# Two masking products side by side: the causal mask of two neighbouring score tiles, put behind the second tile's products

## The chip, the cores and the metric

The kernel runs on one core of one Trainium2 chip. The metric is the device time of one execution in microseconds (us). Five engines take part. TensorE (PE in the profile, PEld for its weight loads) multiplies 128-row tiles from the on-chip memory SBUF and writes the sums to one of eight PSUM banks. VectorE (DVE), ScalarE (ACT) and GpSimd (POOL) do the element-wise work. SyncE (SP) issues most of the DMAs. The engines run by themselves and wait for one another through semaphores.

## The reference, cut to what matters

Two transformer blocks run one after the other on 512 tokens of width 1024. The first block has two layers: a differential attention with an MLP, and a latent ("MLA") attention with an MLP. The second block mixes convolution, pooling and two small attentions, and is not touched here. The two attentions of the first block are what the change is about:

```python
# differential attention, 8 heads; each head has two score matrices (components c = 0, 1)
s = einsum('bqhcd,bkhcd->bhcqk', q_blk, k) * scale
s = where(causal_mask, s, -inf);  p = softmax(s, -1)
a = p[:, :, 0] - lam * p[:, :, 1]          # then a @ v

# latent attention, 8 heads
s = (einsum('bqhd,bkhd->bhqk', qn, k_nope) + einsum('bqhr,bkr->bhqk', qr, k_rope)) * scale
s = where(causal_mask, s, -inf);  p = softmax(s, -1)   # then p @ v
```

Every matrix product is made nearly exact in float32: each operand is split into a high and a low part, and two or three products are summed in one PSUM bank.

## The kernel before, in words

The scores of a head are made as four tiles, one for each block of 128 queries, called A, B, C and D in this document. Because of the causal mask tile `i` needs only the keys of the blocks 0 to `i`, so the tiles are 128, 256, 384 and 512 keys wide (the narrowest is computed 256 wide). Tile `i` of a group goes to PSUM bank `(T + i) % 4`: the four tiles of a group fill four banks, and the next group of four needs each of them again.

A tile of the differential attention is two products (`diff_scores`, L658 and L659) and one masking product (`mask_later`, L645). The masking product multiplies a 128x128 bf16 identity (the weights) by a 128x128 bf16 mask and adds the result to the 128 columns of the tile on the diagonal. It is the last of the tile and raises `tile_done`. A tile of the latent attention is two products L774 and L775, one product in two pieces at L776, and the same masking product (`mla_scores`). The scores are made negated, so that the row maximum is found with a minimum.

What follows a tile is the same in both attentions. VectorE waits for the tile's `tile_done` and takes the row minimum (`negmin`, L1525 in the differential attention, L1717 in the latent one). ScalarE waits for that and takes the exponential (`probs` L1055, `mla_probs` L1202), which also gives the row sum and raises `bank_free` of the tile's bank. TensorE waits for `bank_free` (`bank_ready`, L502) before the first product of the next tile in that bank. `tile_done` counts upwards, tile after tile.

The order of the work on each engine is written out by hand. In the differential attention TensorE does for head n, in `diff_step`: the four tiles of component 0 of head n+1, the turn of an earlier output (L693), the product with v of head n-1 (`weighted`, L683), the transposes of head n's probabilities (L672, which wait for `a_done`, raised by L1546), and the four tiles of component 1 of head n+1. VectorE does for head n: `rinv` and two more small steps (L1535 to L1539), which need the last exponential of the head's component 1; the four row minima of component 0 of head n+1; the combination of the two components (`probs`, L1546); some steps for earlier heads (L1560, L1552, L1555); the four row minima of component 1 of head n+1. ScalarE takes the exponentials, and between them copies the transposed probabilities (L1064) and the outputs (L1071).

In the latent attention (`mla_step`) TensorE does for head n: tiles A and B of head n+1, the transposes of head n (L672), tiles C and D of head n+1, the product with v (L786). VectorE does: `rinv` and the normalisation of head n (L1724, L1728), minima A and B, one step for the head before (L1422), minima C and D. Before head 0 of either attention all its tiles are made in one go. After each attention the output projection follows at once (L534), with weights that are loaded and split long before.

Of the kernel before, what the change touches and what calls it, by code (L numbers as in the profile page):

```python
# [20 lines left out]
P = 128  # L21
# [38 lines left out]
C, T = {}, {}  # L60
# [61 lines left out]
def build(nc, wst, xT, gains, cos, sin, ident_in, mask_in, lam, pT_in, tab_in, buckets_in, pool_w_in, pool_fix_in, outT):  # L122
    ctx = ExitStack()
    with ctx:
        def sem(name):
            return ctx.enter_context(nc.semaphore(name))
# [139 lines left out]
        ps = [ctx.enter_context(nc.psum_tensor(f"ps{b}", [P, S], F32)) for b in range(8)]  # L266
# [9 lines left out]
        tile_done = sem("tile_done")  # L276
# [215 lines left out]
        def _(pe):  # L492
# [6 lines left out]
            def bank_ready(t, per=0, i=0):  # L499

                if not isinstance(i, int) or t // 4 + (per // 4) * i > 0:
                    pe.wait_ge(bank_free[t % 4], t // 4 + (per // 4) * i)  # L502
# [140 lines left out]
            def mask_later(out):  # L643

                return pe.matmul(out, ident_b[:, :], mask_b[:, :], start=False, stop=True)  # L645

            def diff_scores(par, half, comp, first=False):

                pe.wait_ge(stage_full[par][comp], 96 * (half + 1))
                if first:  # L650
                    pe.wait_ge(pad_zero, 2 * par + comp + 1)
                for i in range(QT):
                    n = 8 * par + 4 * comp + i
                    bank_ready(T["diff"] + n, 16, half)
                    b, q = ps[(T["diff"] + n) % 4], slice(P * i, P * i + P)
                    wide = max(P * (i + 1), 2 * P)

                    pe.matmul(b[:, 0:wide], stage[par][:, comp, 0, q], stage[par][:, comp, 1, 0:wide], start=True, stop=False)  # L658
                    pe.matmul(b[:, 0:wide], stage[par][:, comp, 0, q], stage_k_lo[par][comp][:, 0:wide],  # L659
                              start=False, stop=False)  # L660
                    mask_later(b[:, q]).then_inc(tile_done, 1)

            def transposes(src, ready, n):

# [31 lines left out]
            def diff_step(par, half, first=0, scores=True):  # L696

                n = 2 * half + par
                if scores:
                    diff_scores(1 - par, half + par, 0, first=n == 0 if isinstance(n, int) else False)  # L700
                if first >= 3 and scores:
                    turn(o_raw[1 - par], n - 3, X["diff_o"] + n - 3)
                if first >= 1:
                    weighted(pT[1 - par], v_tok, n - 1, n - 1, oc_done)
                if not scores:
                    turn(o_raw[1 - par], n - 3, X["diff_o"] + n - 3)
                transposes(probs[par][:, 0, :], lambda j, i: (a_done, 4 * n + j + 1), n)
                if scores:
                    diff_scores(1 - par, half + par, 1, first=n == 0 if isinstance(n, int) else False)

            pe.wait_ge(dve_const, 5)
            diff_scores(0, 0, 0, first=True)
            diff_scores(0, 0, 1, first=True)
            for n in range(3):
# [18 lines left out]
            c, t = C["dkv"], T["dkv"]  # L733
# [7 lines left out]
            c, t = C["ukv"], T["ukv"]  # L741
# [17 lines left out]
            c, t = C["uq"], T["uq"]  # L759
# [5 lines left out]
            def mla_scores(par, n, tiles):  # L765

                if 0 in tiles:
                    pe.wait_ge(mla_full[par], 80 * (n // 2 + 1) if isinstance(n, int) else 80 + 40 * (n - par))
                for i in tiles:
                    bank_ready(T["mla"] + i, 4, n)  # L770
                    b, w, q = ps[(T["mla"] + i) % 4], P * (i + 1), slice(P * i, P * i + P)
                    wide = max(w, 2 * P)

                    pe.matmul(b[:, 0:wide], mla_qr[par][:, q], mla_kr[:, 0:wide], start=True, stop=False)  # L774
                    pe.matmul(b[:, 0:wide], mla_qr[par][:, q], mla_kr_lo[:, 0:wide], start=False, stop=False)  # L775
                    pe.matmul(b[:, 0:w], mla_qn[par][:, q], k_nope[:, n, 0:w], start=False, stop=False)  # L776
                    mask_later(b[:, q]).then_inc(tile_done, 1)

            def mla_weighted(par, n):

# [9 lines left out]
            def mla_step(par, n, scores=True):  # L790
                if scores:
                    mla_scores(1 - par, n + 1, (0, 1))
                transposes(mla_probs[par], lambda j, i: (pn_done, 4 * n + j + 1), HEADS + n)
                if scores:
                    mla_scores(1 - par, n + 1, (2, 3))
                mla_weighted(par, n)

            pe.wait_ge(kr_zero, 1)
            pe.wait_ge(kr_full, 96)
            mla_scores(0, 0, range(QT))  # L800
            mla_step(0, 0)
            with pe.Fori(0, HEADS // 2 - 1) as i:
# [7 lines left out]
            c, t = C["w_in"], T["w_in"]  # L810
# [1567 lines left out]
```

## Time and profile before

| | us |
|---|---|
| median of 3 runs | 1896.39 |
| lowest, highest | 1894.56, 1898.91 |
| the profiled execution's own time | 1895.68 |
| its span (first to last instruction) | 1893.9 |
| TensorE busy in the span | 1846.5 (97%) |
| mean granted TensorE clock | 0.99 |
| differential attention | from 154.8 to 227.3 of the span |
| latent attention | from 715.2 to 776.6 of the span |

The profile is one execution. Ends of TensorE's instructions are modelled, so distances between the starts of two neighbouring instructions say what one of them costs, not its duration: the products overlap in the array. An idle time in square brackets stands in front of an instruction and names what ended it.

### The profile page before, as it was taken

The numbers are of one execution on the slowest core, as the hardware profiler recorded it, in microseconds if no ns is written. First come the engines' busy times: TensorE is split into PE (matmuls) and PEld (weight loads), VectorE is DVE, ScalarE is ACT, GpSimd is POOL, SyncE is SP. The second block draws the span as 40 slices with busy tenths as digits, with TensorE's granted clock in tenths as the row PEclk, the third lists the DMA queues.
The fourth block names the chain that finished last, engine by engine and source line by source line (L and its number), as shares of the span: only waits on it lengthen the run. The fifth ranks groups of instructions, "written<-read, shape, count | busy, mean of one in ns | idle before, by whom it ended". The sixth has DMA issues, their size and how long they took to land.

```text
span 1893.9 us, 22795 instructions
## 1 busy us (share of the span) xinstructions
PE 1846.5 (97%) x8690; PEld 1504.4 (79%) x8694; DVE 914.5 (48%) x1129; ACT 613.3 (32%) x886; POOL 571.6 (30%) x365
## 2 busy tenths in 40 slices
PE   8999999999999999999999999999998999999988
PEld 6897788888888876788888888777785888888866
DVE  6745763333335765543333335597546332333364
ACT  4236722122223335422212224234435222322342
POOL 3310355141325430252324155221115210211252
PEclk9999999999999999999999999999998999999998
DMA  4434332232222234225232222311121222222221
GB/s 173 142 111 96 96 112 89 89 111 89 98 102 89 89 114 117 91 93 141 89 104 96 89 98 98 121 67 45 45 101 61 95 92 104 93 102 99 89 88 67
DMA packets 40558, 183.94 MB, mean 97 GB/s; under 512 B 5512, under 2 KB 12200, under 8 KB 21416
## 3 DMA queue, kind: packets, MB, share of 16 engines
q1 hardware_dynamic: 38224, 179.26, 28.0%
q10 hardware_dynamic: 2264, 3.72, 1.0%
q8 instruction: 47, 0.77, 0.2%
q14 instruction: 23, 0.19, 0.0%
HBM read 161.99 MB, written 3.67 MB: 87 GB/s over the span
## 4 chain that ended last, share of the span: by engine, by line
PE 86%; DVE 8%; ACT 2%; POOL 2%; issue 1%; DMA 1%; SPq 0%; DVEq 0%; ACTq 0%; POOLq 0%
PE ps L495 23%; PE ps L496 23%; PE ps L497 23%; PE ps L545 3%; PE ps L534 3%; PE ps L535 3%; PE ps L672 1%; DVE xb L1422 1%; PE ps L863 1%; PE ps L881 1%; PE ps L786 1%; PE ps L776 1%; DVE wlo L1416 1%; DVE probs L1546 1%; PE ps L579 1%
## 5 line engine op out<-in xcount | busy, mean ns | idle before, releaser
L1416 DVE TENSOR_TENSOR wlo<-raw,whi 128x2048 fp32r<-128x2048 f32 x142 | 352.1, 2480 | 324.4 <-ACT whi L972 324.0
L972 ACT ACTIVATE whi<-raw 128x2048 fp32r<-128x2048 f32 x149 | 284.3, 1908 | 382.6 <-PE ps L497 272.6
L495 PE MATMUL ps<-xb,whi 128*128 128x512 f32 x1024 | 402.8, 393 | 2.8 <-DVE wlo L1416 1.6
L497 PE MATMUL ps<-xb,wlo 128*128 128x512 f32 x1024 | 400.0, 391 | 0.0
L496 PE MATMUL ps<-xb,whi 128*128 128x512 f32 x1024 | 399.9, 391 | 0.0
L495 PE MATMUL ps<-xa_hi,whi 128*128 128x512 f32 x788 | 308.7, 392 | 3.2 <-DVE wlo L1416 3.2
L497 PE MATMUL ps<-xa_hi,wlo 128*128 128x512 f32 x788 | 307.8, 391 | 0.0
L496 PE MATMUL ps<-xa_lo,whi 128*128 128x512 f32 x788 | 307.7, 390 | 0.0
L495 PEld LDWEIGHTS ps<-xb,whi 128*128 128x128 f32 x1024 | 193.3, 189 | 45.9 <-issue 3.3
L497 PEld LDWEIGHTS ps<-xb,wlo 128*128 128x128 f32 x1024 | 193.1, 189 | 40.8
L496 PEld LDWEIGHTS ps<-xb,whi 128*128 128x128 f32 x1024 | 193.4, 189 | 39.8 <-issue 0.2
L2121 POOL TENSOR_TENSOR u_sq<-u_tmp 128x512 f32<-128x512 f32 x64 | 66.7, 1042 | 385.8 <-DVE u_tmp L1626 385.8
L495 PEld LDWEIGHTS ps<-xa_hi,whi 128*128 128x128 f32 x788 | 148.8, 189 | 35.3 <-DVE wlo L1416 4.5
L497 PEld LDWEIGHTS ps<-xa_hi,wlo 128*128 128x128 f32 x788 | 148.5, 188 | 31.2
L496 PEld LDWEIGHTS ps<-xa_lo,whi 128*128 128x128 f32 x788 | 148.7, 189 | 30.5
L1607 DVE TENSOR_TENSOR h<-ps,h 128x512 f32<-128x512 f32 x80 | 54.0, 690 | 188.8 <-PE ps L497 144.0
L1626 DVE SCALAR_TENSOR_TENSOR u_tmp<-ps,rstd_f 128x512 f32<-128x512 f32 x64 | 43.4, 690 | 143.3 <-PE ps L497 141.5
L2214 POOL TENSOR_TENSOR hid_t<-silu_t,up_t 128x512 f32<-128x512 f32 x22 | 28.3, 1286 | 236.8 <-ACT silu_t L1372 120.5
L534 PE MATMUL ps<-xa_hi,whi 128*128 128x512 f32 x188 | 73.5, 391 | 2.0 <-ACT xa_hi L979 1.9
L535 PE MATMUL ps<-xa_hi,wlo 128*128 128x512 f32 x188 | 73.2, 389 | 0.0
L2124 POOL TENSOR_TENSOR xb<-u_sq,xb 128x512 fp32r<-128x512 f32 x32 | 70.4, 2201 | 2.5
L2124 POOL TENSOR_TENSOR xa_lo<-u_sq,xa_hi 128x512 fp32r<-128x512 f32 x32 | 68.4, 2139 | 2.5
(311 smaller groups left out, 2516.9 us busy)
## 6 DMA issues: line engine op xcount, KB each, us to landing
raw<-wst SPq DMA_DIRECT2D x149, 1024.0 KB, 4.8
stage<-qk_split SPq DMA_DIRECT2D x64, 128.0 KB, 2.4
h<-xT ACTq DMA_DIRECT2D x4, 512.0 KB, 8.0
stage_k_lo<-qk_split SPq DMA_DIRECT2D x32, 64.0 KB, 2.0
mla_qn<-q_nope SPq DMA_DIRECT2D x8, 256.0 KB, 2.7
mla_v<-v_tok SPq DMA_DIRECT2D x8, 256.0 KB, 2.7
outT<-h SPq DMA_DIRECT2D x8, 256.0 KB, 2.0
bias_scratch<-bias_rows ACTq DMA_DIRECT2D x1, 1536.0 KB
```

Source lines behind the costliest of these rows:

```text
L495: pe.matmul(out, lhs_hi, rhs_hi, start=first, stop=False)
L496: pe.matmul(out, lhs_hi, rhs_lo, start=False, stop=False)
L497: return pe.matmul(out, lhs_lo, rhs_hi, start=False, stop=last)
L534: pe.matmul(out, w_hi[:, k, m], xhi[:, k, :], start=(k == 0), stop=False)
L535: pe.matmul(out, w_lo[:, k, m], xhi[:, k, :], start=False, stop=False)
L545: mm = pe.matmul(ps[(t0 + a) % 4][:, :], w_hi[:, k, m], xlo[:, k, :], start=False, stop=(k == kt - 1))
L972: act.activation(whi[slot][:, :], raw[slot][:, :], ACT.Copy).then_inc(whi_done, 1)
L1416: dve.tensor_tensor(wlo[slot][:, :], raw[slot][:, :], whi[slot][:, :].bitcast(F32), ALU.subtract).then_inc(wlo_done, 1)
L1607: dve.tensor_tensor(h[:, k, :], ps[t % 4][:, :], h[:, k, :], ALU.add).then_inc(bank_free[t % 4], 1)
L1626: dve.scalar_tensor_tensor(out=u_tmp[:, a, :], in0=ps[tt % 4][:, :], scalar=0.0, in1=rstd_f[:, :], op0=ALU.max, op1=ALU.mult)\
L2121: pool.tensor_tensor(u_sq[:, a, :], u_tmp[:, a, :], u_tmp[:, a, :], ALU.mult).then_inc(hid_sq, 1)
L2124: pool.tensor_tensor(hlo[:, j, :], u_sq[:, a, :], hhi[:, j, :].bitcast(F32), ALU.subtract)\
```

## The change

The masking product of a tile no longer stands behind the tile's own products. When the products of the second tile of a pair (B, or D) have been issued, a new helper `mask_pair` issues the masking products of both tiles, one behind the other, first A then B (first C then D). Both have the same weights. Each still raises `tile_done` by one, in the same order of tiles. The number of products and of weight loads stays the same. The second tile's wait for its bank now stands ahead of the first tile's masking product. The third kind of place where the identity is used, in the second block, is untouched.

```diff
+            def mask_pair(t, i):
+
+                for j in range(2):
+                    mask_later(ps[(t + j) % 4][:, P * (i + j):P * (i + j) + P]).then_inc(tile_done, 1)
+
             def diff_scores(par, half, comp, first=False):
...
                     pe.matmul(b[:, 0:wide], stage[par][:, comp, 0, q], stage_k_lo[par][comp][:, 0:wide],
                               start=False, stop=False)
-                    mask_later(b[:, q]).then_inc(tile_done, 1)
+                    if i % 2 == 1:
+                        mask_pair(T["diff"] + n - 1, i - 1)
...
                     pe.matmul(b[:, 0:w], mla_qn[par][:, q], k_nope[:, n, 0:w], start=False, stop=False)
-                    mask_later(b[:, q]).then_inc(tile_done, 1)
+                    if i % 2 == 1:
+                        mask_pair(T["mla"] + i - 1, i - 1)
```

The order on TensorE, in the differential attention: the four tiles of component 1 of head 2, which follow the transposes of head 1 (`stage` holds the queries and the high part of the keys, `stage_k_lo` the low part). Before:

```order
L658 MATMUL ps<-stage_97 128x256 [waits bank_free0,stage_full01]
L659 MATMUL ps<-stage_k_lo_100,stage_97 128x256
L645 MATMUL ps<-mask_b,ident_b 128x128
L658 MATMUL ps<-stage_97 128x256 [waits bank_free1]
L659 MATMUL ps<-stage_k_lo_100,stage_97 128x256
L645 MATMUL ps<-mask_b,ident_b 128x128
L658 MATMUL ps<-stage_97 128x384 [waits bank_free2]
L659 MATMUL ps<-stage_k_lo_100,stage_97 128x384
L645 MATMUL ps<-mask_b,ident_b 128x128
L658 MATMUL ps<-stage_97 128x512 [waits bank_free3]
L659 MATMUL ps<-stage_k_lo_100,stage_97 128x512
L645 MATMUL ps<-mask_b,ident_b 128x128
```

The same place of the changed kernel, whose lines are 5 further down:

```order
L663 MATMUL ps<-stage_97 128x256 [waits bank_free0,stage_full01]
L664 MATMUL ps<-stage_k_lo_100,stage_97 128x256
L663 MATMUL ps<-stage_97 128x256 [waits bank_free1]
L664 MATMUL ps<-stage_k_lo_100,stage_97 128x256
L645 MATMUL ps<-mask_b,ident_b 128x128 x2
L663 MATMUL ps<-stage_97 128x384 [waits bank_free2]
L664 MATMUL ps<-stage_k_lo_100,stage_97 128x384
L663 MATMUL ps<-stage_97 128x512 [waits bank_free3]
L664 MATMUL ps<-stage_k_lo_100,stage_97 128x512
L645 MATMUL ps<-mask_b,ident_b 128x128 x2
```

The masks of tiles A and C have moved behind two more products and behind the wait for the next bank; the masks of B and D stand where they stood.

On TensorE in the latent attention, tiles C and D of head 1, with the rows taken away and put in (`k_nope` and `mla_kr` are the keys, `mla_qr` the rotated part of the queries, bank numbers shown):

```order
+L780 MATMUL ps1<-mla_kr_168,mla_qr1_167 128x384 [waits bank_free1]
+L781 MATMUL ps1<-mla_kr_lo_169,mla_qr1_167 128x384
+L782 MATMUL ps1<-k_nope_158,mla_qn1_165 128x384
+L780 MATMUL ps2<-mla_kr_168,mla_qr1_167 128x512 [waits bank_free2]
+L781 MATMUL ps2<-mla_kr_lo_169,mla_qr1_167 128x512
+L782 MATMUL ps2<-k_nope_158,mla_qn1_165 128x512
 L645 MATMUL ps1<-mask_b_68,ident_b_67 128x128
-L774 MATMUL ps2<-mla_kr_168,mla_qr1_167 128x512 [waits bank_free2]
-L775 MATMUL ps2<-mla_kr_lo_169,mla_qr1_167 128x512
-L776 MATMUL ps2<-k_nope_158,mla_qn1_165 128x512
 L645 MATMUL ps2<-mask_b_68,ident_b_67 128x128
```

The mask of tile C (bank `ps1`) now follows all of tile D's products (bank `ps2`), and the two masks are neighbours. On the other engines no instruction moves.

## Rows read from the trace of the kernel before

**Rows 1.** The page: busy us, share of the span, instructions.

```profile
PE 1846.5 (97%) x8690; PEld 1504.4 (79%) x8694; DVE 914.5 (48%) x1129; ACT 613.3 (32%) x886; POOL 571.6 (30%) x365
```

**Rows 2.** Waits, differential attention, 154 to 225: total us, times, longest.

```profile
DVE negmin L1525 <- PE ps L645: 5.3, 10, 1.8
```

**Rows 3.** Waits, latent attention, 712 to 772.

```profile
DVE negmin L1717 <- PE ps L645: 19.7, 23, 1.5
```

**Rows 4.** Timeline of TensorE, head 3: start us, us, engine, line, operation.

```profile
183.11 0.23 PE L645 MATMUL ps<-mask_b,ident_b 128*128 128x128 bf16 x1
183.15 0.36 PE L658 MATMUL ps<-stage 128*128 128x256 f32 x1
183.35 0.28 PE L659 MATMUL ps<-stage_k_lo,stage 128*128 128x256 f32 x1
...
183.95 0.23 PE L645 MATMUL ps<-mask_b,ident_b 128*128 128x128 bf16 x1
...
184.54 0.23 PE L645 MATMUL ps<-mask_b,ident_b 128*128 128x128 bf16 x1
```

**Rows 5.** Timeline of TensorE, first score tile, no mask ahead of it.

```profile
154.84 0.28 PE L658 MATMUL ps<-stage 128*128 128x256 f32 x1
154.95 0.28 PE L659 MATMUL ps<-stage_k_lo,stage 128*128 128x256 f32 x1
```

**Rows 6.** Timeline of VectorE and ScalarE, head 3, tiles C and D.

```profile
184.22 0.56 DVE L1525 TENSOR_REDUCE negmin<-ps 128x1 f32<-128x384 f32 x1
184.81 0.69 DVE L1525 TENSOR_REDUCE negmin<-ps 128x1 f32<-128x512 f32 x1
185.53 0.69 ACT L1055 ACTIVATE probs<-ps,negmin 128x512 f32<-128x512 f32 x1
```

**Rows 7.** Timeline of TensorE and VectorE, head 5, tiles C and D.

```profile
201.54 0.23 PE L645 MATMUL ps<-mask_b,ident_b 128*128 128x128 bf16 x1
...
201.39 0.55 DVE L1525 TENSOR_REDUCE negmin<-ps 128x1 f32<-128x384 f32 x1
...
201.85 0.68 DVE L1525 TENSOR_REDUCE negmin<-ps 128x1 f32<-128x512 f32 x1
```

**Rows 8.** Timeline, head 0, tile D of component 1, and its minimum.

```profile
158.33 0.50 PE L658 MATMUL ps<-stage 128*128 128x512 f32 x1
...
158.90 0.23 PE L645 MATMUL ps<-mask_b,ident_b 128*128 128x128 bf16 x1
...
159.17 0.69 DVE L1525 TENSOR_REDUCE negmin<-ps 128x1 f32<-128x512 f32 x1 [0.39 <-PE ps L645]
```

**Rows 9.** Timeline, transposes of head 0, and weight loads (PEld) of head 3's last ones.

```profile
163.31 0.59 PE L672 MATMUL ps<-ident,probs 128*128 128x128 f32 x3 [1.77 <-DVE probs L1546]
...
190.60 0.42 PEld L672 LDWEIGHTS ps<-ident,probs 128*128 128x128 f32 x4 [0.34 <-DVE probs L1546]
```

**Rows 10.** Stretches: length; PE, PEld, DVE, ACT, POOL busy; PEclk; DMA share, GB/s.

```profile
164.00:169.00 5.00, 4.79 (x23) 3.75 (x24) 2.22 (x6) 2.83 (x9) 0.00 (x0) 0.66 0.66 149
170.00:222.00 52.00, 49.82 (x358) 39.71 (x357) 43.31 (x110) 41.29 (x133) 16.30 (x16) 1.00 0.59 141
```

**Rows 11.** Timeline of TensorE, latent attention, transposes of a steady head.

```profile
743.60 1.60 PE L672 MATMUL ps<-ident,mla_probs 128*128 128x128 f32 x10
```

**Rows 12.** Timeline of VectorE, latent attention, the normalisation ahead of those transposes.

```profile
742.05 0.55 DVE L1728 TENSOR_SCALAR mla_probs<-mla_probs,rinv 128x256 f32<-128x256 f32 x2
```

**Rows 13.** Timeline, latent attention, last head: tiles C and D, then transposes.

```profile
768.16 0.22 PE L645 MATMUL ps<-mask_b,ident_b 128*128 128x128 bf16 x1
...
769.59 0.22 PE L645 MATMUL ps<-mask_b,ident_b 128*128 128x128 bf16 x1
...
769.85 0.69 DVE L1717 TENSOR_REDUCE negmin<-ps 128x1 f32<-128x512 f32 x1 [0.88 <-PE ps L645]
...
772.01 1.70 PE L672 MATMUL ps<-ident,mla_probs 128*128 128x128 f32 x10
```

**Rows 14.** Timeline of TensorE, latent attention, transposes of its head 0.

```profile
721.38 1.63 PE L672 MATMUL ps<-ident,mla_probs 128*128 128x128 f32 x10 [0.46 <-DVE mla_probs L1728]
```

## The prediction

> **What bounds the kernel now.** The first view to read is the busy time of the engines: TensorE is busy for 97% of the span and the next engine for 48% [rows 1]. As a rule, then, a nanosecond of TensorE is a nanosecond of the kernel. The waits of the two attentions are the second view, because there the rule may fail. In the differential attention VectorE waits 10 times for a masking product, 5.3 us in all [rows 2]; in the latent one 23 times, 19.7 us [rows 3]. Such a wait costs nothing if VectorE has time to spare, and all of it if TensorE later waits for VectorE. The timelines tell which. In the differential attention TensorE's transposes wait for VectorE's combination of the probabilities: 1.77 us at head 0, and at head 3 the weight loads of the last four still stand idle for 0.34 us [rows 9]. The loop there is closed by this chain: combination, last transposes, component 1's tiles, minima, exponentials, minima of the next head, combination. In the latent attention's steady heads the combination's counterpart, the normalisation, starts at 742.05, and the transposes that read it start at 743.60 without a wait [rows 11, 12]: TensorE is the bound, with over a microsecond of slack on the other side. Its two ends are different. TensorE waits 0.46 us for the first head's probabilities [rows 14], and the last head's transposes at 772.01 follow at once on a chain that begins at the mask of tile D, 769.59 [rows 13].
>
> **What the edit gives TensorE.** In head 3 a mask starts at 183.11 and the next tile's first product 0.04 later, at 183.15; its second product starts 0.20 after that, at 183.35 [rows 4]. Without a mask ahead, the same two products start 0.11 apart, 154.84 and 154.95 [rows 5]. So a mask that has a float32 tile behind it takes 0.04 + 0.09, about 0.12 us since the rows are rounded: most of it is the next weight load, which the short mask cannot cover. After the edit one of each pair's masks has the other mask behind it. No row shows what such a slot costs. Its ends are 0.04 (the start after a mask above) and 0.12 (a float32 load as badly covered as now). I take 0.06: it has half the columns of the products that start 0.11 apart [rows 5], and its weights have half the width. The gain is 0.12 - 0.06 = 0.06 us for each pair that lies on TensorE's path, with ends 0 and 0.08.
>
> The TensorE page of the Trainium skill ("TensorE: Matmul & The Clock Gate", Weight-path perf modes) says that weights which are not float32 are loaded by a faster way, which speaks for the low end. Its section on the back-to-back issue gap gives some 81 ns for a stream of loads and products of 128 columns; as an estimate by that page the gain would be 0.04 us a pair, and the sum below 0.3 us higher. No run here shows it yet.
>
> **What the edit takes from the chain behind the tiles.** The mask of tile C moves behind tile D's products. In head 3 mask D starts at 184.54. Before it stand three masks, at 0.12 each; after the edit the mask of C stands behind A's and B's alone, at 0.06 + 0.12. So it starts at 184.54 - 0.36 + 0.18 = 184.36, against 183.95 now, and mask D at 184.42. The minimum of tile C starts 0.27 after its mask, now 184.22 [rows 6], then 184.63. The minimum of D cannot start sooner than 0.46 after C's (201.39 to 201.85, where nothing is waited for, [rows 7]): 185.09, against 184.81 [rows 6]. The exponential of tile D, at 185.53, starts 0.03 after that minimum ends, and everything behind it is late by the same 0.28 us: `rinv`, the minima of the next head, the combination, the transposes. The masks of A and B have slack, since ScalarE is still copying when A's minimum is done.
>
> In head 5 VectorE is later for reasons of its own and the delay smaller: mask D at 201.54 puts mask C at 201.54 - 0.18 = 201.36, its minimum at 201.63, against 201.39: 0.24 us [rows 7]. Heads 2 and 3 are of the first kind. Head 4 comes out between, 0.27. Heads 5, 6 and 7 are of the second. The sum of the six is 0.28 x 2 + 0.27 + 0.24 x 3 = 1.55 us.
>
> Head 0 has both its components exposed. Component 0 is late by 0.28 as above, and with it the bank that tile D of component 1 waits for: its first product goes from 158.33 to 158.61. From there to a mask it is 158.90 - 158.33 = 0.57, so mask C starts at 159.18, its minimum at 159.45 and D's at 159.91, against 159.17 [rows 8]: 0.74 us. The component 0 tiles of the later heads cost nothing: VectorE reads them only after `rinv`.
>
> Head 1's component 1 runs at half clock. The granted clock is 0.66 in the mean of 164 to 169 [rows 10], so TensorE ran at 1.2 instead of 2.4 GHz for some 3.4 of these 5 us, after it had stood idle for 1.77 us. If that stretch stays where it is in time, work that comes 0.74 us later does up to half of that, 0.37, less of itself in it. Against this stands head 1's own delay of 0.24. I take 0, with ends -0.1 and +0.3.
>
> In the latent attention the end of the last head is a straight chain. Mask D at 769.59 becomes mask C at 769.59 - 0.12 = 769.47; its minimum starts 0.26 later and D's 0.46 after that, at 770.19, against 769.85 [rows 13]: 0.34 us, and the transposes, the product with v and the output projection all move with it. The first head ends in the same chain and TensorE waits for it already [rows 14]: 0.34 again. In the steady heads the same 0.34 goes into the slack [rows 11, 12] and costs nothing; with the slack gone it would cost 0.34 for each of six heads. Of the 16 pairs 13 lie on TensorE's path (not the last pairs of the first and the last head, nor the one behind which TensorE waits), and give 13 x 0.06 = 0.78. The sum is 0.68 - 0.78 = -0.1 us, with ends -0.4 and +0.7.
>
> DMAs, and the waits of SyncE for `tile_done`, hang on the last tile of each group, whose mask moves by 0.1 us at most. No queue is passed. Behind both attentions TensorE is the bound and nothing takes the delay back.
>
> **The sum.** 0.74 + 0 + 1.55 - 0.1 = 2.2 us. The profiled execution took 1895.68, so it would take 1897.9. The median of the runs is 0.71 above that: 1896.39 + 2.2 = 1898.6 us, or 0.12% more.
>
> **The rivals.**
>
> First, the delay is absorbed: VectorE and ScalarE find the time again somewhere in a head. The idle 0.34 before the last transposes [rows 9] speaks against it, since it says who waits for whom; for it speaks that only 5.3 us of waits for masks are seen [rows 2]. Then what remains is TensorE's gain, 0.8 to 1 us in the latent attention and perhaps as much in the other: 1895.1.
>
> Second, on the far side: a further stretch at half clock. TensorE is already idle for 1.77 us before the first transposes and drops to 1.2 GHz behind it [rows 9, 10]. The edit lengthens the idle pieces around heads 0 and 1. One more stretch of 3.4 us loses up to 3.4 / 2 = 1.7 us, two lose 3.4: 1900.3 to 1902. It decides as soon as one of the idle pieces outside that stretch grows enough to bring the clock down; from 170 to 222 the granted clock is 1.00 throughout, so the short pieces there do not do so now [rows 10]. The same page of the skill warns, in its section on psum-queue depth-cycling, of a clock that oscillates when TensorE idles briefly and often between groups of products. The trace shows none of it from 170 to 222.
>
> Third, the change does not do what it says: both masks have the same weights, but the second weight load stays in the program, and a pair may save nothing. Then the latent attention costs 0.7 instead of -0.1, the mask of C comes 0.06 later throughout, and the sum is 2.2 + 0.8 + 0.5 = 3.5: 1899.9.
>
> **How the numbers follow.** The forecast, a small loss of 1.5 to 3 us, gets 0.64; absorbed 0.12; a further half-clock stretch 0.12; no saving 0.08; something else 0.04. A measurement of this kernel tells about 0.2%, 3.8 us, from no change. "Slower by over 0.2%" takes two thirds of the clock rival, a quarter of the third and the upper tail of the forecast, since the runs of before alone lie 4 us apart: 0.08 + 0.02 + 0.09, with the rest of something else 0.21. "Faster by over 0.2%" would need 3.8 us, while all 48 pairs at their best give 48 x 0.08 = 3.8: 0.03. The range runs from the absorbed case to nearly two lost clock stretches, 1895.0 to 1901.6.
>
> **What would show it right or wrong.** In the profile after, the two neighbouring masks should start 0.06 apart, and the first product of tile D 0.18 rather than 0.22 after C's second one. The minimum of tile C should start some 0.4 later after its head's first product than now, that of D some 0.25 to 0.3. From the first score tile to the output projection the differential attention should take about 74.8 us instead of 72.5, the latent one 61.3 instead of 61.4. The first figure falls if ScalarE's exponential of D starts no later in its head than now. The second falls if the transposes of steady heads begin to wait. The sum falls if the granted clock shows more stretches at half than now, or fewer.

## The result and the profile after

The changed kernel takes 1899.23 us in the median of 20 runs (1897.89 to 1900.83), the kernel before 1896.48 in the same jobs (20 runs, 1894.56 to 1898.91). The medians are 2.75 us apart. The ratio is 1.0016, with a 95% interval of 1.0009 to 1.0022, which is 1.7 to 4.2 us. The forecast of a small loss (1898.6 us, within 0.2% of before) came out. The terms of its sum did not all do so, and the experiments below are about them. The two executions that were profiled took 1895.68 us (before) and 1900.14 us (after), so the profiles lie further apart than the medians.

The page of the changed kernel, against [rows 1], looks the same. Nothing can be learnt from it.

```profile
PE 1849.2 (97%) x8694; PEld 1506.4 (79%) x8694; DVE 912.3 (48%) x1129; ACT 612.8 (32%) x886; POOL 571.2 (30%) x365
```

The waits do change. First VectorE's for a mask in the differential attention (154 to 226 us; total us, times, longest), against [rows 2], then in the latent one (714 to 775), against [rows 3], and behind them the three largest waits of TensorE's weight loads in the differential attention:

```profile
DVE negmin L1532 <- PE ps L645: 8.4, 12, 2.2
...
DVE negmin L1724 <- PE ps L645: 20.6, 9, 2.7
...
PEld ps L663 <- ACT probs L1062: 8.6, 21, 0.8
PEld ps L678 <- DVE probs L1553: 6.0, 13, 1.9
PEld ps L645 <- issue: 4.4, 16, 0.3
```

The same rows of the kernel before for the weight loads read:

```profile
PEld ps L672 <- DVE probs L1546: 7.3, 17, 1.9
PEld ps L645 <- issue: 7.1, 32, 0.3
PEld ps L658 <- ACT probs L1055: 2.4, 7, 0.5
```

VectorE's wait for masks grew in both stages. In the first one TensorE's loads then stand 6.2 us longer behind the banks that ScalarE frees, and 1.3 us less behind `probs` and 2.7 us less ahead of the masks: 2.2 us more idle time of the loads, though not every part of it stops the products.

Head 3 of the changed kernel (start us, us, engine, line, operation), against [rows 4] and [rows 6]:

```profile
184.88 0.36 PE L663 MATMUL ps<-stage 128*128 128x256 f32 x1
185.08 0.28 PE L664 MATMUL ps<-stage_k_lo,stage 128*128 128x256 f32 x1
185.20 0.28 PE L663 MATMUL ps<-stage 128*128 128x256 f32 x1
...
185.44 0.29 PE L645 MATMUL ps<-mask_b,ident_b 128*128 128x128 bf16 x2
185.53 0.42 PE L663 MATMUL ps<-stage 128*128 128x384 f32 x1
185.79 0.34 PE L664 MATMUL ps<-stage_k_lo,stage 128*128 128x384 f32 x1
185.97 0.39 PE L663 MATMUL ps<-stage 128*128 128x512 f32 x1
...
186.44 0.29 PE L645 MATMUL ps<-mask_b,ident_b 128*128 128x128 bf16 x2
```

```profile
186.70 0.56 DVE L1532 TENSOR_REDUCE negmin<-ps 128x1 f32<-128x384 f32 x1 [0.37 <-PE ps L645]
187.18 0.68 DVE L1532 TENSOR_REDUCE negmin<-ps 128x1 f32<-128x512 f32 x1
...
187.89 0.69 ACT L1062 ACTIVATE probs<-ps,negmin 128x512 f32<-128x512 f32 x1
```

The group's first product starts at 182.78 in before and at 184.88 here. Measured from it, mask C comes at 1.56 us, before at 1.17; its minimum at 1.82, before 1.44; D's minimum at 2.30, before 2.03; the exponential at 3.01, before 2.75. So tile C is 0.38 to 0.39 later in its head, and everything from D's minimum on 0.26 to 0.27.

Where the stages end is read from three rows of TensorE: the output projection behind the differential attention, the latent attention's first score product, and the projection behind that. Before:

```profile
227.28 0.48 PE L534 MATMUL ps<-xb,whi 128*128 128x512 f32 x1
...
715.19 0.28 PE L774 MATMUL ps<-mla_kr,mla_qr 128*128 128x256 f32 x1
...
776.63 0.48 PE L534 MATMUL ps<-xa_hi,whi 128*128 128x512 f32 x1
```

and after, with the first score product ahead of them:

```profile
155.75 0.28 PE L663 MATMUL ps<-stage 128*128 128x256 f32 x1
...
229.69 0.48 PE L534 MATMUL ps<-xb,whi 128*128 128x512 f32 x1
...
717.58 0.28 PE L780 MATMUL ps<-mla_kr,mla_qr 128*128 128x256 f32 x1
...
778.94 0.47 PE L534 MATMUL ps<-xa_hi,whi 128*128 128x512 f32 x1
```

| us | before | after | difference | forecast |
|---|---|---|---|---|
| ahead of the first score product | 154.84 | 155.75 | +0.91 | 0 |
| differential attention | 72.44 | 73.94 | +1.50 | +2.3 |
| between | 487.91 | 487.90 | 0 | 0 |
| latent attention | 61.44 | 61.35 | -0.09 | -0.1 |
| behind it | 1117.26 | 1119.40 | +2.14 | 0 |
| span | 1893.9 | 1898.3 | +4.4 | +2.2 |

Two thirds of the difference between these two profiles lie in stages whose code the change does not touch. Of these the stretch ahead of the first score product is within its spread: the same code takes from 153.07 to 156.20 us there in the fourteen profiles of this document. The part behind the latent attention needs a closer look, which comes below. A table by stage is therefore worth more here than the time, and each experiment below is read by it first. "diff" and "latent" stand for the second and fourth row.

### The profile page after: what moved, and what is told of

Same layout as the page of the kernel before. It is cut to its first block, busy times and chain, and to the rows that moved or that the text cites. A ratio compares the mean times of both kernels' runs of the same rounds, so it can differ in the third digit from the quotient of the medians.

```text
span 1898.3 us, 22799 instructions
## 1 busy us (share of the span) xinstructions
PE 1849.2 (97%) x8694; PEld 1506.4 (79%) x8694; DVE 912.3 (48%) x1129; ACT 612.8 (32%) x886; POOL 571.2 (30%) x365
## 4 chain that ended last, share of the span: by engine, by line
PE 87%; DVE 7%; ACT 2%; POOL 2%; issue 1%; DMA 1%; SPq 0%; ACTq 0%; DVEq 0%; POOLq 0%
PE ps L495 23%; PE ps L496 23%; PE ps L497 23%; PE ps L545 3%; PE ps L534 3%; PE ps L535 3%; PE ps L678 1%; DVE xb L1429 1%; PE ps L870 1%; PE ps L888 1%; PE ps L782 1%; PE ps L793 1%; DVE wlo L1423 1%; PE ps L579 1%; POOL rstd_t L2067 1%
```

## Experiments

### One stage at a time, and the pairs put elsewhere

**e1** keeps the pairs in `mla_scores` alone, **e2** in `diff_scores` alone.

```diff
 (e1, in diff_scores)
-                    if i % 2 == 1:
-                        mask_pair(T["diff"] + n - 1, i - 1)
+                    mask_later(b[:, q]).then_inc(tile_done, 1)
```

> Pairs of masks in the latent attention alone; the differential attention as before. My theory (0.057 us gained by TensorE for each of 13 pairs, 0.35 us lost at each end): the latent attention takes 61.35 us against 61.44 of before, the differential one 72.4, and the time is that of before within 0.3 us of -0.1. The rival that the change costs something outside the two stages: the time is 1 us or more above that of before although both stages show nothing.

> Pairs of masks in the differential attention alone. My theory: the differential attention takes 73.9 us against 72.4 of before, the latent one 61.4, and the time is 1.5 us above that of before. Rival, that the measured 2.75 us have a part outside both stages: the time is 2.5 us or more above, with the same 1.5 in the stage.

e1: diff 72.09, latent 61.36; median 1895.78 against 1896.83, ratio 0.9997 (0.9988 to 1.0006). e2: diff 74.07, latent 61.45; 1899.21, ratio 1.0011 (1.0002 to 1.0020). The loss is the differential attention's, and the latent attention's small gain is there in the profile (61.35 to 61.36 in e1, in after and in its repetition **e5**, 61.44 to 61.45 in every kernel with the old latent order and nothing ahead of it), far below what the time can tell. e2's stage is 1.6 us longer, as its theory said. Its median is 2.4 us above that of before, between the 1.5 of the theory and the 2.5 of the rival, so the time does not decide between them.

**e3** leaves the pairs only where, by the prediction, nobody waits: component 0 of the heads behind the first, and in the latent attention all but the last two tiles of the first and last head. For this the last round of the loop over heads is written out.

```diff
+                    if comp == 1 or alone:
+                        mask_later(b[:, q]).then_inc(tile_done, 1)
+                    elif i % 2 == 1:
+                        mask_pair(T["diff"] + n - 1, i - 1)
...
+                    if i >= 2 and isinstance(n, int) and n in (0, HEADS - 1):
+                        mask_later(b[:, q]).then_inc(tile_done, 1)
...
-            with pe.Fori(0, HEADS // 2 - 1) as i:
+            with pe.Fori(0, HEADS // 2 - 2) as i:
...
+            mla_step(1, HEADS - 3)
+            mla_step(0, HEADS - 2)
```

> Pairs only where no chain hangs on the first mask: component 0 of heads 1 to 7 in the differential attention, and all of the latent attention but the C and D tiles of its first and last head. My theory: the differential attention keeps its 72.4 us (within 0.2), the latent one loses both its ends' costs and takes 61.44 - 0.057 x 13 = 60.7 us; the time is 0.7 us below that of before. The rival, that a late mask costs wherever it stands: the differential attention takes 0.7 us more, half of what the whole change costs it.

**e4** pairs the masks of tiles A and B alone, in both attentions:

```diff
+                    if i == 1:
+                        mask_pair(T["diff"] + n - 1, 0)
+                    elif i >= 2:
+                        mask_later(b[:, q]).then_inc(tile_done, 1)
```

> Only tiles A and B are paired, in both attentions; C and D as before. My theory (mask C is what is late): the differential attention takes no more than 72.4 us, perhaps 0.3 less since mask C comes 0.06 earlier; the latent one 61.44 - 0.057 x 7 = 61.0. The rival, that mask A is late too: the differential attention takes 0.2 us more for each head, 1 us or more in all.

e3: diff 72.07, latent 61.10; 1895.68, ratio 0.9994 (0.9985 to 1.0003). e4: diff 70.91, latent 61.01; 1896.06, ratio 0.9996 (0.9987 to 1.0005). In both the loss of the differential attention is gone. In e4 heads 2 and 3 step by 7.95 us (from the exponential of tile D in one head to that in the next), where they step by 8.03 in before and 8.30 in the changed kernel: the pair of A and B gives a little in these heads, and the pair of C and D takes it and more. So the pair of C and D is the cause, and with the rows of head 3 above this is the delay of tile C. The 70.91 is not a gain of the edit: its profile has no stretch at half clock in head 1, and e9 below, with the old order and no such stretch either, takes 70.88. In e4 TensorE waits three times, 3.3 us in all, for the DMA that brings the low part of the keys, and in e9 not once, so nothing of what A and B gave in the first heads is seen at the stage's end. The last of the three:

```profile
208.31 0.38 PE L663 MATMUL ps<-stage 128*128 128x256 f32 x1 [0.89 <-DMA stage_k_lo<-qk_split]
```

The latent stage of e4 gives the expected 61.0. That of e3 misses its 60.7: the heads written out of the loop run 7.48 and 7.41 us where the same heads ran 7.24 and 7.31 in the loop. So the heads written out took 0.3 us more. In the second of them TensorE waits 0.21 us for ScalarE's copy of the transposed probabilities (758.89 us in e3), which it does not do in e1; why was not tested.

**e6** goes the other way and puts all four masks of a differential group behind tile D.

```diff
+                for j in range(4):
...
+                    if i == 3:
+                        mask_pair(T["diff"] + n - 3, 0)
```

> All four masks of a group behind tile D, in the differential attention alone; the latent attention as before. My theory: the masks of A and B are now late too, and the minima start with A's after all products: about 0.7 us later at the exponential of D, and the minima of component 0 another 0.3 late, since they can start only when its tile D is made. So some 0.9 us for each of heads 1 to 7 less what is absorbed, and 2 for head 0: the differential attention takes 78 to 81 us and the time is 6 to 9 us above that of before. The rival, that the loss comes from the longer wait for a bank ahead of the mask and is paid once: 76 us or less.

diff 78.75, latent 61.45; 1903.81, ratio 1.0041 (1.0029 to 1.0054). Stage and time agree here: +6.3 us and +7.2. VectorE's waits for masks are 14.0 us in e6 (152 to 226), against 8.4 with pairs and 5.3 before, and the heads from head 2 on step by 9.0 to 9.1 us, about 1 us more than before in heads 2 and 3 and 0.3 to 0.8 more in the later ones:

```profile
DVE negmin L1531 <- PE ps L645: 14.0, 16, 2.9
```

### Where 0.24 us a head went: GpSimd and a small step of VectorE

By when the exponential of tile D starts in component 1, with the same origin in each head, the changed kernel is later than before by 0.93, 0.91, 1.18, 1.45, 1.77, 1.74, 1.81 and 1.81 us in heads 0 to 7. At the stage's end it is 1.50. So heads 2 to 4 add 0.27 to 0.32 each as forecast, and heads 5 to 7 nothing instead of 0.24 each. Inside those heads the delay is there (the exponential of D starts 3.02 us behind the group's first product, before 2.78). Something behind the exponentials gives it back. In the kernel before, VectorE's combination begins with `coef`, a step on 4 columns. Heads 3 and 5, and GpSimd at the second (start, length):

```profile
186.56 0.22 DVE L1537 SCALAR_TENSOR_TENSOR coef<-rinv,neg_lam,rowsum 128x4 f32<-128x4 f32 x1
...
203.59 0.54 DVE L1537 SCALAR_TENSOR_TENSOR coef<-rinv,neg_lam,rowsum 128x4 f32<-128x4 f32 x1
...
203.07 1.04 POOL L2092 TENSOR_TENSOR sq_tmp<-o_raw 128x512 f32<-128x512 f32 x1
```

The same step takes 0.54 us where GpSimd squares an output at the same time, and both end within 0.02 us of each other (204.13 and 204.11). So it is in heads 4, 6 and 7. Over the eight heads of before it takes 221, 222, 223, 224, 489, 537, 533 and 541 ns. In the changed kernel everything ahead of it is later, and GpSimd's square is nearly over:

```profile
206.24 0.29 DVE L1544 SCALAR_TENSOR_TENSOR coef<-rinv,neg_lam,rowsum 128x4 f32<-128x4 f32 x1
...
205.48 1.04 POOL L2099 TENSOR_TENSOR sq_tmp<-o_raw 128x512 f32<-128x512 f32 x1
```

That is the longest of the eight; the others take 221 to 232 ns. A shorter `coef` makes the next head's tiles sooner, and head by head this is the missing term: 0.27 less in head 4 against the 0.24 of head 5 (measured -0.03), 0.25 less in head 5 (head 6: +0.07), 0.31 less in head 6 (head 7: 0), and 0.31 less in head 7 (the tail: -0.3). To test it, GpSimd's square is cut to a quarter of its width (the mean square made from it is then not the right one), in the kernel before (**e7**) and in the changed one (**e8**).

```diff
-                    pool.tensor_tensor(o_sq[:, :], o, o, ALU.mult).then_inc(sqo_done, 1)
+                    pool.tensor_tensor(o_sq[:, 0:P], o[:, 0:P], o[:, 0:P], ALU.mult).then_inc(sqo_done, 1)
```

> The kernel before, with GpSimd's square of the output (o_sq, 128x512) cut to its first 128 columns; the other columns stay zero, so the mean square that is computed from them is not the right one. My theory: in the heads 4 to 7 of before, VectorE's small step coef, which takes 0.22 us in heads 0 to 3 and 0.49 to 0.54 there, waits for the end of this GpSimd operation. With a short one it takes 0.22 everywhere and the differential attention takes 0.3 less for each of three or four heads: 71.4 us against 72.4. The rival, that coef is slow there for another reason: 0.5 us again and 72.4.

> The changed kernel with the same short square (three quarters of the square are left out). My theory: what the change cost less than I had said, in heads 5 to 7 and in the tail, was hidden by coef's wait; without that wait the pairs cost 0.24 us in each of these heads too, and the differential attention takes 2.2 to 2.5 us more than the run with the short square alone (against 1.5 with the full one). The rival, that the delay is absorbed elsewhere: 1.5 us again.

In e7, head 5:

```profile
203.72 0.40 POOL L2093 TENSOR_TENSOR sq_tmp<-o_raw 128x128 f32<-128x128 f32 x1
...
204.24 0.22 DVE L1538 SCALAR_TENSOR_TENSOR coef<-rinv,neg_lam,rowsum 128x4 f32<-128x4 f32 x1
```

`coef` is back at 0.22 in all heads. diff is 71.42 in e7 (1.02 less than before, with a stretch at half clock in head 1 in either; the median 1895.72, ratio 0.9994, 0.9985 to 1.0004) and 73.91 in e8 (as in the changed kernel; 1899.89, ratio 1.0019, 1.0009 to 1.0029, with one single run of 2070.55 us whose reason I can't name). By when the exponential of tile D starts, e8 is later than e7 by 0.90, 0.88, 1.15, 1.42, 1.76, 1.98, 2.31 and 2.59 us in heads 0 to 7: now heads 5 to 7 add their 0.22 to 0.33 too. So without this effect the pairs cost 73.91 - 71.42 = 2.49 us in this stage, and with it 1.50. The prediction had 2.3. The times of the whole kernel say nothing finer than that e7 is like before and e8 like the changed kernel.

The Trainium skill ("SBUF — State Buffer", Who interferes with whom) says that a VectorE instruction with two inputs in SBUF and a GpSimd instruction that reads SBUF exclude each other, and that the later one waits for the whole of the other. `coef` has `rinv` and `rowsum` as inputs, both in SBUF, and the rows agree: its start is recorded at 203.59, and it ends 0.02 us behind GpSimd. That it is this port, and not another resource of the two engines, no run here shows.

### Is it the chain, or only where the later work falls in time?

**e5** is the changed kernel again, **e12** the kernel before again, **e9** and **e10** the kernel before with 24 or 48 masks more, ahead of the latent attention, into a bank that is written anew afterwards.

```diff
+            for _ in range(24):
+                pe.matmul(BC[:, 0:P], ident_b[:, :], mask_b[:, :], start=True, stop=True)
```

> The changed kernel once more, for the spread of its stages. My theory: the differential attention takes 73.9 us again when its half-clock stretch of 3.4 us is there, and some 1.5 less without; the latent one 61.35. The rival, that the whole 2.75 us measured are made in the stages: 75 us or more in the differential attention.

> The kernel before once more, for a second profile of its stages. My theory: the differential attention takes 72.1 to 72.4 us with its half-clock stretch and some 1.3 less without; the part behind the latent attention lies anywhere from 1117 to 1120 us. The rival: 1117.2 us behind the latent attention as in the first profile, so that the 1119.4 of the changed kernel's profiles are its own.

> The kernel before, with 24 more masking products, one behind the other, into a bank that nobody reads, ahead of the latent attention (their result is overwritten). It measures two things. First, the slot of a mask behind a mask: my theory is 0.057 us, so 24 take 1.4 us between the two attentions. Second, what a plain delay of 1.4 us in the middle of the program does to the measured time: by my theory it adds 1.4 us, as the pairs' 1.3 to 1.5 should; by the rival (the half-clock stretches of the later stages fall at other places and last longer after such a delay) it adds 2.5 to 3.

> The same with 48 masks, 2.7 us. My theory: the time is 2.7 us above that of before. The rival: the stretches depend on where the delay leaves the program, so the addition is off from 2.7 by 1 us or more, to either side.

| | diff | latent | behind it | median us | ratio (95%) |
|---|---|---|---|---|---|
| before | 72.44 | 61.44 | 1117.26 | | |
| e12 | 72.15 | 61.45 | 1120.18 | 1897.56 | 1.0003 (0.9993 to 1.0012) |
| after | 73.94 | 61.35 | 1119.40 | 1899.23 | 1.0016 (1.0009 to 1.0022) |
| e5 | 73.73 | 61.36 | 1119.25 | 1899.91 | 1.0018 (1.0008 to 1.0027) |
| e9 | 70.88 | 61.52 | 1117.69 | 1897.98 | 1.0015 (1.0006 to 1.0024) |
| e10 | 72.48 | 61.52 | 1118.14 | 1899.83 | 1.0017 (1.0008 to 1.0026) |

First the masks themselves, the 24 of e9 in one row:

```profile
715.00 1.51 PE L799 MATMUL ps<-mask_b,ident_b 128*128 128x128 bf16 x24
```

One alone is recorded with 0.22 to 0.23 us [rows 13], so 23 further ones take 1.29: 0.056 us for each, what the prediction took (0.06). In the changed kernel two masks are recorded in one row of 0.29, again 0.06 more than one.

Then the part behind the latent attention. After the first two profiles it looked as if 1119.4 belonged to the changed kernel: the changed kernel, e2 and e5 had 1119.25 to 1119.40, the kernel before 1117.26. e12 refutes that it is the changed kernel's alone: the very kernel before has 1120.18 in another profile, and e1, whose differential attention is that of before, has 1120.29. The part takes 1117.2 to 1120.3 us in the fourteen profiles, with the same code in all. Its stretches at half clock lie in different places and add up to 29 to 36 us, and its length follows their sum: three profiles with 29 us take 1117.2 to 1117.7, four with 32 to 33 take 1118.1 to 1118.3, seven with 36 take 1119.3 to 1120.3. For instance from 1205 to 1265 (length; PE, PEld, DVE, ACT, POOL busy; PEclk; DMA share, GB/s), in before, in e12 and in after:

```profile
1205.00:1265.00 60.00, 57.59 (x292) 44.23 (x291) 46.65 (x118) 20.26 (x32) 18.42 (x4) 1.00 0.25 89
```

```profile
1205.00:1265.00 60.00, 58.15 (x280) 44.49 (x279) 45.82 (x115) 18.52 (x31) 18.37 (x4) 0.94 0.25 86
```

```profile
1205.00:1265.00 60.00, 58.15 (x287) 44.60 (x286) 45.47 (x111) 20.45 (x32) 18.46 (x4) 0.97 0.22 74
```

TensorE's granted clock was full throughout in the first and not in the two others. So the code of before can do what the changed kernel does. But it doesn't do it equally often: all four profiles with pairs of C and D in both components (after, e2, e5, e8) are among the seven with 36 us, and only three of the ten others (e1, e4, e12).

Fourteen profiles are few, but for every execution, profiled in full or not, the record gives TensorE's mean granted clock over the span, to three digits. Sorted by it, these are 103 executions of the kernel before (those that e1 to e12 were compared with, and e12 itself) and 30 of the changed kernel (after and e5):

| mean granted clock | before: executions, mean us | changed: executions, mean us |
|---|---|---|
| 0.986 | 0 | 2, 1900.7 |
| 0.987 | 0 | 9, 1900.4 |
| 0.988 | 29, 1898.2 | 13, 1899.2 |
| 0.989 | 35, 1896.9 | 6, 1898.5 |
| 0.990 | 37, 1895.6 | 0 |
| 0.991 | 2, 1894.4 | 0 |

The means are 0.9891 and 0.9878. Over 1900 us this is some 5 us more at 1.2 instead of 2.4 GHz, one and a half stretches of 3.4 us. A step of 0.001 goes with 1.3 us in the kernel before, so the lower clock stands for about 1.7 us of the difference. At the same reading the changed kernel is 1.0 (at 0.988) to 1.6 us (at 0.989) slower: that is about the stage's 1.5. The lower clock goes with the pairs of C and D in both components of the differential attention: e2 has 0.9880, e8 0.9874 against 0.9885 in e7, and e6, with all four masks behind, 0.9882 in six executions, while e1, e3, e4 and e11 together (44 executions) have 0.9892. So something in this does belong to the change, though the two profiles of before taken by themselves do not show it. Why the pairs bring it is not shown.

Can a plain delay do the same? e9 adds 23 x 0.056 plus the first mask's slot, 1.4 us by that count (1.65 between the two stages in its profile). Its median is 1.34 above that of before, but its mean is 2.15 above and its ratio says 2.8 (1.1 to 4.6): six of its eleven executions lie at 1897.6 to 1898.0 and five at 1899.2 to 1900.9. Its mean granted clock is 0.9883, against 0.9892 of before in the same job. e10 adds 2.7; its median is 3.2 above, its mean 2.95, its clock 0.9889. So e10 agrees with 1 to 1, and e9 decides neither for 1 to 1 nor for its rival of 2.5 to 3. A delay in the middle may by itself change how much is run at half clock, and the changed kernel's lower clock may be of this kind.

The stretch at half clock in the differential attention is one more such place. From 162 to 170 in after, in e4 and in e9:

```profile
162.00:170.00 8.00, 5.98 (x29) 4.44 (x29) 4.59 (x13) 5.23 (x18) 0.00 (x0) 0.79 0.58 133
```

```profile
162.00:170.00 8.00, 7.55 (x54) 5.80 (x53) 5.81 (x16) 6.13 (x22) 0.00 (x0) 1.00 0.63 144
```

```profile
162.00:170.00 8.00, 5.75 (x34) 3.81 (x34) 5.93 (x15) 6.25 (x21) 0.00 (x0) 1.00 0.59 135
```

e9's code up to this place is the kernel before's, yet it has no stretch and its stage takes 70.88 instead of 72.1 to 72.5. So the kernel before has this stretch in some executions and not in others; it costs 1.2 to 1.6 us. Ahead of it TensorE stands idle for 0.34 and then 1.77 us in before, and for 0.53, 0.64 and 1.73 in the changed kernel. All four profiles that have the change's pairs of C and D in both components (after, e2, e5, e8) have the stretch, and six of the eight with the old order of C and D have it. If the changed kernel has it always and the kernel before in about three quarters of its executions, this is worth a quarter of 1.5, 0.4 us on the medians. Four profiles cannot establish an always, and it would be a quarter of a stretch where the granted clocks ask for one and a half; the rest must lie in other stages.

### What the experiments propose

**e11** takes what each place showed: A and B paired everywhere, C and D only in latent heads 1, 2, 4 and 6, whose slack covers it and which need no code out of the loop.

```diff
+                    if i == 1 or i == 3 and pair_cd:
+                        mask_pair(T["mla"] + i - 1, i - 1)
+                    elif i >= 2 and not pair_cd:
+                        mask_later(b[:, q]).then_inc(tile_done, 1)
...
+            mla_step(0, 0, pair_cd=True)
...
+                mla_step(1, 2 * i + 1, pair_cd=True)
```

> The pairs where they can only gain: A and B in both attentions, and C and D in the latent attention's heads 1, 2, 4 and 6. My theory: differential attention 72.0 or less (70.9 if its half-clock stretch is absent, as in the run with A and B alone), latent 61.44 - 11 x 0.057 = 60.8; the time is 1 us below that of before, 0.05%. The rival: no difference to the kernel before.

The latent stage takes 60.81 us, the shortest of all. diff is 72.25, with the stretch. The median is 1896.26 against 1896.64, ratio 0.9996 (0.9987 to 1.0005): half a microsecond of gain is in the latent stage's profile, and cannot be told from nothing in the time. In the differential attention no gain is seen: the old order takes 72.09 to 72.48 with the stretch.

## Why the prediction was right, and where it was not

**The price of a mask.** Right: 0.06 was taken, and two neighbouring masks start 0.056 us apart in the latent attention (e1) and 0.067 in the differential one (e2). The first product of tile D starts 0.18 behind C's second one, as forecast (185.79 to 185.97). The rival "saves nothing" is out. The Trainium skill's 81 ns for a stream with 128 columns ("TensorE: Matmul & The Clock Gate", Back-to-back issue gap) would have given 0.04 a pair; the trace does not agree with it for these products.

**The delay of tile C and D inside a head.** Right to 0.03 us (C +0.38 for 0.41, D and its exponential +0.26 to +0.27 for 0.28, and +0.24 in heads 5 to 7).

**Head 0.** The mechanism was right, the term too small: +0.93 where 0.74 stood. The missing 0.19 is in component 0. Tile D of that first group (start us, us; the idle time before it and what ended it in brackets):

```profile
156.84 0.50 PE L663 MATMUL ps<-stage 128*128 128x512 f32 x1
...
156.84 0.19 PEld L663 LDWEIGHTS ps<-stage 128*128 128x128 f32 x1 [0.25 <-ACT v_tok L1043]
```

ScalarE is still copying `v_tok` out of the bank that tile D wants. The product starts 1.09 behind the first instead of 1.00 (0.18 behind C's second one), its own weight load is no longer covered, and its second product follows 0.34 later (157.18), in head 3 0.23. The prediction moved the masks and kept the rest of the group in place; it did not ask what frees the bank of a tile that comes sooner.

**Heads 2 to 7.** +0.27, +0.27 and +0.32 in heads 2 to 4 stood against 0.28, 0.28 and 0.27. The terms of heads 5 to 7 are the step that failed: +0.24 each was forecast, -0.03, +0.07 and 0 came, and the way to the stage's end gave back 0.3 more. The row that says so was in the trace of before: `coef` takes 0.22 us in one half of the heads and 0.54 in the other. "VectorE is later for reasons of its own" was said of head 5, and those reasons were not followed up. e7 and e8 show this term: 1.0 us.

**Head 1** at half clock took nothing in these two profiles (its step is 9.58 in before and 9.57 after): the 0 that was chosen. But with the stretch in it the same step is 9.27 in e12 and 9.36 in e5, so the code of before alone varies by 0.3 us here, and the 0 is not resolved better than that.

**The latent attention.** -0.09 for -0.1, and by its parts: the steady heads step by 7.281 instead of 7.394 us, two pairs of 0.06 each; the longer waits of VectorE there (20.6 us in all) cost nothing. The last head's chain, against [rows 13]:

```profile
771.50 0.28 PE L645 MATMUL ps<-mask_b,ident_b 128*128 128x128 bf16 x2
...
772.23 0.68 DVE L1724 TENSOR_REDUCE negmin<-ps 128x1 f32<-128x512 f32 x1
...
774.38 0.33 PE L678 MATMUL ps<-ident,mla_probs 128*128 128x128 f32 x1 [0.39 <-DVE mla_probs L1735]
```

From the pair of masks to D's minimum is 0.73 us, as forecast (0.26 + 0.46), and the transposes now wait 0.39 where they followed at once (0.34 forecast).

**The rivals.** "Absorbed" was half true in four heads, by a mechanism that it didn't name. "A further stretch at half clock" appears in no profile of the changed kernel from 170 to 224, where it was looked for. Over the whole kernel it came: one and a half stretches more in the mean of the executions, most of it outside the differential attention.

**The sum.** The stages came to +1.4 us, not +2.2, and the medians differ by 2.75 (1.7 to 4.2). So 1898.6 was near 1899.23 partly by luck: one term was too large by 1 us, and 1.3 us came from elsewhere. The record names the elsewhere: a lower granted clock, about 1.7 us by the count above, a term that the sum put at nothing. "Behind both attentions TensorE is the bound and nothing takes the delay back" asked whether the late part gives time back, not whether it takes more. 0.4 of it may be the stretch in head 1. Why the change lowers the clock stays open; e9 leaves it possible that any delay of this size does.

## To carry to other kernels

Moving a small instruction behind its neighbour's work to save its own slot pays only where nobody behind it waits: here 0.06 us a pair against 0.3 us a head. Read the consumer's chain of the stage first and pair only the tiles with slack (A and B here, C and D in the steady latent heads). When a step of fixed size has two durations in one profile, find out what it shares time with, because a delay may cost nothing on it, or double. Where the effect is a microsecond or two in 1900, compare the stage between two fixed instructions, in several profiles of either kernel, before looking at the total. Then sort all executions by their mean granted clock: what is left at the same reading is about the change's own path, and the rest goes with the clock.

## What the runs showed of the hardware

A VectorE step on 128x4 elements takes 0.22 us alone and up to 0.54 beside a GpSimd multiplication of 1.04 us, with both ending together; with the multiplication at 0.40 us and over before it starts, it takes 0.22.

A bf16 product of 128 columns, with its own weight load, takes 0.056 us in a row of 24. Between a float32 product of 256 columns and the next one lie 0.11 us (154.84 to 154.95 [rows 5]), and 0.20 where a bf16 mask stands ahead of the first (183.15 to 183.35 [rows 4]).

The same instructions run 1117.2 to 1120.3 us behind the latent attention, by how much of that is at half clock (29 to 36 us), and one stretch in head 1, worth 1.2 to 1.6 us, comes or stays away in the same code.

A change of 1.5 us in one stage came with a mean granted clock of 0.9878 instead of 0.9891 in the whole kernel, 1.7 us more.
